# Two-layer four-mixer block: norms worked token tile by token tile, products around them reordered, both layers in one block

## The reference, cut to what matters

```
h = rmsnorm(x, n_pre_mix); proj = h @ w_in          # 1024 columns -> the branch inputs and gates
y_a .. y_d = four mixers (gated delta rule, dilated window attention, stick-breaking attention, retention)
mixed = (g_a*y_a + g_b*y_b + g_c*y_c + g_d*y_d) @ w_o
x = x + rmsnorm(mixed, n_post_mix)
h2 = rmsnorm(x, n_pre_mlp)
f = square(relu(h2 @ w_mlp_in)) @ w_mlp_out         # 1024 -> 4096 -> 1024
x = x + rmsnorm(f, n_post_mlp)
```

## Time and profile before

| what | value |
|---|---|
| median of three runs | 2524.46 us |
| the profiled execution: its own time | 2526.41 us |
| its span, first to last instruction | 2524.5 us |
| TensorE, share of the span | 95% |
| GpSimd, VectorE, ScalarE | 52%, 38%, 30% |
| mean granted TensorE clock | 0.979 of full speed |
| moved by DMA | 197.54 MB, mean 78 GB/s |

### The profile page before, as it was taken

The page is one execution under the profiler, slowest core; times in us unless marked ns, Lnnn a source line. Parts: engine busy times, 40 slices in busy tenths (PEclk is TensorE's granted clock), DMA queues, the critical chain, the costliest instruction groups (busy, mean ns, idle before and its releaser), DMA issues. The chain is left out here.

```text
span 2524.5 us, 29523 instructions
## 1 busy us (share of the span) xinstructions
PE 2386.9 (95%) x11488; PEld 1939.3 (77%) x11488; DVE 953.0 (38%) x1236; ACT 748.3 (30%) x1360; POOL 1319.0 (52%) x748
## 2 busy tenths in 40 slices
PE   7999999999998989999789999999999988999996
PEld 6798876777776768888677988768777766788885
DVE  4662325434634431123246632255246254212222
ACT  4434225222135121122144442351222341211221
POOL 4512653555643646677455126436555435566773
PEclk9999999999999999999999999999999999999998
DMA  4201321322221323322032013213222213232221
GB/s 158 84 26 34 92 84 50 108 83 86 63 70 44 104 80 93 100 93 99 26 110 84 18 43 92 75 50 117 75 88 68 69 44 100 84 96 96 97 95 50
DMA packets 107492, 197.54 MB, mean 78 GB/s; under 512 B 8528, under 2 KB 20816, under 8 KB 106960
## 3 DMA queue, kind: packets, MB, share of 16 engines
q1 hardware_dynamic: 106192, 189.27, 24.5%
q10 hardware_dynamic: 1152, 6.29, 0.7%
HBM read 193.44 MB, written 2.10 MB: 77 GB/s over the span
## 5 line engine op out<-in xcount | busy, mean ns | idle before, releaser
L507 POOL TENSOR_SCALAR ring_hi<-stage 128x1024 fp32r<-128x1024 f32 (+2 forms) x372 | 383.2, 1030 | 1137.8 <-PE big L1476 1085.2
L509 POOL TENSOR_TENSOR ring_lo<-stage,ring_hi 128x1024 fp32r<-128x1024 f32 (+2 forms) x372 | 936.8, 2518 | 31.0
L1476 PE MATMUL big<-h_hi,ring_hi 128*128 128x512 f32 (+1 forms) x1776 | 703.8, 396 | 4.2 <-POOL ring_lo L509 1.7
L1476 PE MATMUL big<-h_hi,ring_lo 128*128 128x512 f32 (+1 forms) x1776 | 693.6, 391 | 0.0
L1476 PE MATMUL big<-h_lo,ring_hi 128*128 128x512 f32 (+1 forms) x1776 | 693.6, 391 | 0.0
L1476 PEld LDWEIGHTS big<-h_hi,ring_hi 128*128 128x128 f32 (+1 forms) x1776 | 334.4, 188 | 81.2 <-issue 6.7
L1476 PEld LDWEIGHTS big<-h_lo,ring_hi 128*128 128x128 f32 (+1 forms) x1776 | 333.9, 188 | 71.6
L1476 PEld LDWEIGHTS big<-h_hi,ring_lo 128*128 128x128 f32 (+1 forms) x1776 | 334.3, 188 | 70.3 <-issue 1.9
L1476 PE MATMUL big<-ring_hi,h_hi 128*128 128x512 f32 x768 | 299.7, 390 | 6.2 <-DVE scr L1032 6.2
L1476 PE MATMUL big<-ring_lo,h_hi 128*128 128x512 f32 x768 | 298.8, 389 | 0.0
L1476 PE MATMUL big<-ring_hi,h_lo 128*128 128x512 f32 x768 | 298.8, 389 | 0.0
(11 more groups left out here) (239 smaller groups left out, 2434.8 us busy)
## 6 DMA issues: line engine op xcount, KB each, us to landing
stage<-in_w_in SPq DMA_DIRECT2D x168, 512.0 KB, 3.6
stage<-in_w_mlp_in SPq DMA_DIRECT2D x64, 512.0 KB, 3.8
stage<-in_w_mlp_out SPq DMA_DIRECT2D x64, 512.0 KB, 3.5
stage<-in_w_o SPq DMA_DIRECT2D x16, 512.0 KB, 3.5
stage<-in_w_br_a SPq DMA_DIRECT2D x8, 512.0 KB, 3.7
stage<-in_w_br_c SPq DMA_DIRECT2D x8, 512.0 KB, 3.5
stage<-in_w_br_d SPq DMA_DIRECT2D x8, 512.0 KB, 3.5
stage<-in_w_br_b SPq DMA_DIRECT2D x8, 512.0 KB, 3.4
```

The source lines that it names most:

```text
L507: nc.gpsimd.tensor_scalar(rH[jw][0:pp, r, 0:kk, 0:job.n], w, 1.0, 0.0, ALU.mult, ALU.add).then_inc(sem("w_hi"), 1)
L509: nc.gpsimd.tensor_tensor(rL[jw][0:pp, r, 0:kk, 0:job.n], w, f32(rH[jw][0:pp, r, 0:kk, 0:job.n]), ALU.subtract).then_inc(sem("w_ready"), 1)
L1476: ins_ = MM(o_, a_, r_, start=s0, stop=s1)
```

## The change

1. **One block.** The two layers are written out one after the other for every engine (`sync_layer`, `gpsimd_layer`, `scalar_layer`, `vector_layer`, `tensor_layer`). Semaphores are no longer cleared: `upto(name, count)` adds a fixed number per layer. Weights of layer 1 are loaded and split while layer 0 ends. Rotation matrices and most constants are loaded behind the first four weight units; the first DMAs are the identity, token tiles 0 and 1 and the small weights.
2. **Products by token.** `o1` and the last four units of `dn1` run with the token tile outermost: tile 0 through all four units, then tile 1, 2, 3. The output tiles of `o` and `dn` for tokens 0 and 1 lie in the big banks (o0 tile 0 in bank 0, o1 tile 0 in 1, o0 tile 1 in 2, o1 tile 1 in 3), those for tokens 2 and 3 in the mix banks.
3. **Norm chains by token tile.** Square, root, weighting (in PSUM), residual, square of x, root and split follow each other for one token tile of 128 tokens, and the next one's follow behind; the split takes 128 columns at a time.
4. **Scaled transposes.** The scaled copy `hn` is gone. TensorE multiplies the x block (float32) by a diagonal matrix `turn` of the tokens' roots, which VectorE makes from the identity, and so transposes and scales at once.
5. **Halves.** `aq` and `up0` run first for tokens 0 to 255 (products of 256 columns) through all four units, then for tokens 256 to 511.
6. **Output** is stored in four DMAs, one per token tile, each behind that tile's residual.
7. **Fills** of the window loop move from steps 1, 3, 5, 8 to 0, 1, 3, 6.

```diff
+    by_token(*[("pre1", t, hf) for t in range(2) for hf in range(2)])
     for j in JOBS:
+        if j.name in BY_TOKEN:
+            if j.name[-1] == "0":
+                by_token(*[(j.name[:-1] + str(hf), t) for t in range(2) for hf in range(2)])
+            if j.name == "o1":
+                by_token(*[("pre2", t, hf) for t in range(2) for hf in range(2)])
+            continue
...
+            def turned(tag, t):
+                pe.wait_ge(*upto(f"{tag}_dg", t + 1))
+                for hf in range(2):
+                    ps = tile_of((tag, t, hf))
+                    for q in range(4):
+                        k = 4 * hf + q
+                        i = MM(ps[:, q * P:(q + 1) * P], xv[:, t, k * P:(k + 1) * P], turn[:, t, :], start=True, stop=True)
+                    done(i, (tag, t, hf))
+            def normed(tag, t, i):
+                if i % 2:
+                    big_freed(pe, (tag, t, i // 2))
+                else:
+                    pe.wait_ge(*upto(f"{tag}_lo", 6 * t + 3 * (i // 2) + 2))
+            def halves(name, tag, turns):
+                for i in range(4):
+                    normed(tag, 1, i)
+                    for two in ((0, 1), (2, 3)):
+                        unit(job, i, two, slice(0, 2 * P))
+                        for t in turns.get((i, two[0]), ()):
+                            turned(tag, t)
+                for i in range(4):
+                    normed(tag, 3, i)
+                    unit(job, i, None, slice(2 * P, S))
+            def by_token(name, first_unit, tag, need=None):
+                for t in range(NT):
+                    for i in range(first_unit, len(job.units)):
+                        unit(job, i, (t,))
+                        if i == first_unit and t >= 2 and tag:
+                            turned(tag, t - 2)
...
             do("o0", lambda i: pe.wait_ge(*upto("m_lo", 2 * i + 2)))
-                do("o1")
-                pre("pre2")
-                for g in range(8):
-                    do(f"up{g}", None if g else pre_split("pre2"))
+            by_token("o1", 0, "pre2")
+            halves("up0", "pre2", {(0, 0): (2,), (2, 0): (3,)})
+            for g in range(1, 8):
+                do(f"up{g}")
...
-                    if i in (1, 3, 5, 8):
+                if i in (0, 1, 3, 6):
                     fill(1)
...
+            halves("aq", "pre1", {(0, 0): (2,), (2, 0): (3,)} if l else {(1, 2): (2, 3)})
...
+            def after_products(name, tag, ntag, nw, last):
+                for t in range(NT):
+                    y_square(name, 1, t, tag, 4)
+                    y_root(tag, t)
+                    if last:
+                        continue
+                    if t:
+                        split_hi(ntag, nw, t - 1, range(4))
+                    x_square(name, t, ntag)
+                    x_root(ntag, t)
+                    if t:
+                        split_hi(ntag, nw, t - 1, range(4, 8))
+            def diagonal(tag, t):
+                newton(p_y, p_t, p_h, tag, t)
+                TS(turn[:, t, :], ident, p_y[:, t:t + 1], None, ALU.mult).then_inc(sem(f"{tag}_dg"), 1)
...
+                for t in range(NT):
+                    for hf in range(2):
+                        big_freed(sp, (f"dn{hf}", t))
+                    sp.dma_start(x_out[:, t, :], xv[:, t, :]).then_inc(stored, 16)
```

More of the change, by code:

```diff
@@ L293, in mixer_keys @@
     k += [("bf", t) for t in range(5)]
-    k += [("pre2", i) for i in range(KT)]
+    k += [(f"o{hf}", t) for t in (2, 3) for hf in range(2)]
+    k += [("pre2", t, hf) for t in (2, 3) for hf in range(2)]
+    k += [(f"dn{hf}", t) for t in (2, 3) for hf in range(2)]
     return k
@@ L320, in hybrid_kernel @@
         lw = sb("lw", LEND)
-        st = sb("st", 320)
+        st = sb("st", 328)
         scr = sb("scr", 19968)
@@ L407, in sem, with upto @@
             return sems[name]
+        layer = [0]
+        def upto(name, count):
+            return sem(name), count + layer[0] * PER_LAYER.get(name, 0)
         x_loaded = [ctx.enter_context(nc.semaphore(f"x_loaded{t}")) for t in range(NT)]
+        ident_loaded = ctx.enter_context(nc.semaphore("ident_loaded"))
         consts_loaded = ctx.enter_context(nc.semaphore("consts_loaded"))
@@ new lines, in gpsimd_layer @@
+        def gpsimd_layer(pool, l):
+            layer[0] = l
+            for u, (job, i) in enumerate(UNITS):
+                r0, rows = job.units[i]
+                n = u + l * len(UNITS)
+                s, r = n % STAGES, n % RING
+                pp, kk = min(rows, P), max(rows // P, 1)
+                pool.wait_ge(sem(f"w_loaded{s}"), 16 * (n // STAGES + 1))
+                if u >= RING or l:
+                    pool.wait_ge(*upto("w_used", u - RING + 1))
+                w, jw = stg[job.width][0:pp, s, 0:kk, 0:job.n], job.width
+                nc.gpsimd.tensor_scalar(rH[jw][0:pp, r, 0:kk, 0:job.n], w, 1.0, 0.0, ALU.mult, ALU.add).then_inc(sem("w_hi"), 1)
+                pool.wait_ge(*upto("w_hi", u + 1))
+                nc.gpsimd.tensor_tensor(rL[jw][0:pp, r, 0:kk, 0:job.n], w, f32(rH[jw][0:pp, r, 0:kk, 0:job.n]),
+                                        ALU.subtract).then_inc(sem("w_ready"), 1)
@@ L1484, in do @@
-                def do(name, need=None, between=None):
-                    job = JOB[name]
-                    for i in range(len(job.units)):
-                        if need:
-                            need(i)
-                        unit(job, i)
-                        if between:
-                            between(i)
-                fills = []
-                def fill(n=1):
-                    for _ in range(n):
-                        if fills:
-                            unit(*fills.pop(0))
@@ L1502, in half_fill @@
-                def half_fill(t):
-                    unit(*(fills[0] if t == 0 else fills.pop(0)), (t,))
-                def set_fill(*names):
-                    assert not fills
-                    fills.extend((JOB[name], i) for name in names for i in range(len(JOB[name].units)))
-                order = iter([key for key in MIX if key[0] != "raw"])
-                def tile_of(key):
-                    assert next(order) == key, key
-                    b, k = MIX[key]
-                    if k > 1:
-                        pe.wait_ge(sem(f"mix_free{b}"), k - 1)
-                    return mxb[b]
```

2668 lines of the change are left out of this document (1375 added, 1293 removed), and 5 rows, old and new, of the table PER_LAYER.

## The result

The changed kernel took 2504.55 us (median of three runs, 2502.1 to 2505.26; a fourth run, disturbed to 12331.92 us, is left out), the kernel before beside it 2524.74. The ratio is 0.9918, with a 95% interval of 0.9899 to 0.9938. It is faster by 20.2 us at the medians, 0.8%, and that is clear of the scatter. Forecast were 40.2 us and a time of 2484.3 us; the measured time lies above the range of 2470 to 2502. In the profiled executions the span fell from 2524.5 to 2502.7 us; this execution took 2504.55 us in all.

The account below looks back on a forecast made before the run. TensorE, busy 95% of the span, was taken as the bound, with 137.6 us of rest to win. Terms 16.8 + 18.6 - 0.4 + 12.0 - 9.4 + 5.6 = 43.2, less 3.0, gave 40.2 us gained: 2484.3 us, range 2470 to 2502.

Parts of the forecast that it names:

- End: After the last product: residual and store by token tile take 7.5 us against 19.4, 12.0 us gained.
- o0's banks: At o0: new banks make TensorE wait 6.1 us for yb1's last tile, clock falls; 9.4 us lost over both layers.
- Rival C: Banks of o0 harmless, no clock lost or VectorE frees sooner, fills give their full 4; near 2477 us, chance 0.17.
- Fills: Window loop: moved fills remove a 2.06 us wait and its low clock; 2.8 us gained per layer, 5.6 in all.
- Mid-layer: Between o1 and up0: tile chains hide under products, 9.2 us against 17.6; 8.4 us gained per site, 16.8 in all.
- Boundary: Between the layers: same chain, no loop end, table load or repeated loads; 8.9 us against 27.5, 18.6 us gained.
- Launch: Kernel start: first product 4.7 us earlier, but transposes, halves and waits follow; 0.4 us lost.
- Margin: Taken off the sum: 1 us per site for late units or a held-up VectorE step, 3.0 us.
- Rival B: The ring: first slot returns only after the last tile's products, up0 and aq wait 5.3 us a site; near 2501, chance 0.08.
- Rival D: Slower: GpSimd's weight splits stretch VectorE's SBUF work in tiles 2 and 3, 15 us a site; 2530 us, chance 0.03.
- Rival A: At the sites: the chain by tile is longer than its cover, three sites lose 24 us; near 2508, chance 0.15.

Follow-up runs that it names:

- the fills' own run: Changed kernel with the window loop's fills back at rounds 1, 3, 5 and 8: 2508.18 us, ratio 0.9943 to the kernel before.
- the last kernel above: Changed kernel with all cures: o and pre2 banks reordered, one-element steps rewritten, launch root before tile 2's square, 20 products of ones first; 2464.80 us.
- the kernel with the diagonal on ScalarE: Changed kernel with newton's steps taking one tensor and per-partition numbers, and the diagonal made by ScalarE: 2494.76 us, ratio 0.9890 to the kernel before.

## Why the prediction was wrong, and the step that failed

The prediction had the mechanism of the gain and the sign, but the sum was some 20 us too large and the time fell outside the range. By its own steps, each from the profiled executions:

- **End, 12.0 us:** 12.9 measured from the last product on (19.4 less 6.5). Right. Counted from up1's first product in layer 1, it is 11.3 (334.8 us for 346.1): dn1 by token waits 0.88 us for the ring again, at 2478.20, and the prediction had this wait only in the boundary.
- **o0's banks, 9.4 us lost:** 5.89 and 5.87 us of wait, for the 6.1 worked out, where 3.1 stood before. Behind the wait nine products took 3.8 us instead of 2.0, so the clock cost some 1.7 us where the prediction had chosen 2.0. That is 4.5 us a layer and 9.0 together. Right, and the part of the change with the cheapest cure, one line. Rival C, harmless banks, is out.
- **Fills, 5.6 us:** 3.0 and 3.3 us in the two layers of the fills' own run. Right.
- **Mid-layer, 8.4 us a site:** 2.2 measured. This is the step that failed. Its transposes (6.8 us for 7.2) and halves (1.35 for 1.2) were right; its wait was 4.56 us instead of 0.8, and 2.7 us of slow clock came behind it. The step said that the diagonals of tiles 1 to 3 are ready 2 to 3 us before TensorE comes. For tile 2 three steps that take 0.7 us together took 5.2 beside GpSimd, which starts just then, since `o1` by token gives its ring slots back at the last tile. With up0's bank out of the way the diagonal was 1.83 us late; the bank, which the prediction had at 0.8, made 4.56 of it.
- **Boundary, 18.6:** 14.7 measured, from up1's first product to the first product of L1699 (394.0 us; 408.7 before, to L1545). The same three steps took 1.77, 0.97 and 2.47 us there.
- **Launch, 0.4 us lost:** 6.4 lost. The second turned tile was expected at 11.0 and came at 16.02. Tile 2's load, behind whose square the root of tile 1 stands on ScalarE, landed near 10.2 where the prediction estimated 8.6: some 1.5 us. Then newton and the diagonal of tile 1 took 0.74, 0.96 and 2.47 us beside GpSimd: 3.5 us. GpSimd begins at 8.97 instead of 13.54 because its load now comes sooner; the prediction had this load at 7.4 and did not ask what runs beside the split. An earlier load started the engine that holds the chain. The transposes were reckoned at full clock, 1.8 us each, and took 3.78.
- **Margin, 3.0 us,** for a VectorE step held up or a late unit: the mid-layer sites, the boundary and the launch missed 12.4, 3.9 and 6.0 us, together 22.3, seven times the margin.

The measured terms add up to 20.4 us, with 5.4 for the fills as these two executions have them. The profiled executions differ by 21.9. The other 1.5 us lie in stretches that the change does not touch, where the traces scatter.

Rival B, the ring, is out: up0's first unit was split at 891.53, when o1 ended at 891.67. The small pieces of the split did not decide anything in the layers either: L1116 takes 0.34 us a piece, as worked out.

With the one-element steps in their other form most of this comes back: the site by 6.1 us to 8.3 (8.4 forecast), the boundary by 2.7 to 17.4 (18.6), the launch by 4.1 us to 2.3 lost (0.4). So one uncounted mechanism is nearly all of the miss. That this kernel's 2484.29 us stands beside the forecast of 2484.3 so closely is luck: the launch still loses 1.9 us more than forecast, the boundary gains 1.2 less, the margin of 3.0 us was not needed, and the traces scatter by more than all of these. The launch's rest is not the slow transposes alone, since the last kernel above has them at full rate and its first product comes no sooner.

Rival D had named the mechanism and its place, tiles 2 and 3 beside GpSimd, and was kept out of the sum with a chance of 0.03, as a catastrophe of 45 us. It was there, at two fifths of the size (18 us). The argument against it was wrong: that one-column steps are short. A step that stands until the neighbour's instruction ends costs what is left of that instruction, up to 2.4 us, however short it is itself. The rows for this stood before the prediction: L1049 at 680 to 2893 ns and L509 with a median of 2397; the difference between the two ends of L1049 is 2.2 us, close to one GpSimd instruction. And the trace of the kernel before has a small step that is held, a VectorE step of 128x2 that takes 0.17 us alone and here ends with GpSimd's instruction:

```profile
729.27 1.05 POOL L507 TENSOR_SCALAR ring_hi<-stage 128x1024 fp32r<-128x1024 f32 x1 [8.16 <-PE big L1476]
729.48 0.88 DVE L1363 TENSOR_SCALAR st<-st 128x2 f32<-128x2 f32 x1
```

Rival A's price (2508) was near the time, and the chain was longer than its cover, as it says; but the cause was a hold of single steps and not the number of hand-overs.

## What to carry to other kernels

When a chain is moved under other work, ask for each of its steps which instruction will run beside it on GpSimd, and take a VectorE step with two tensors in SBUF, or a wide one from SBUF alone, at the whole length of that instruction; write steps of one element per partition with one tensor and per-partition numbers. A small step is not a short one: 128x2 steps were held as well. Give banks to a new job in the order in which the job before frees them, and ask the same of the next job's first tile. A rival that is a matter of degree belongs in the sum at its likely size, not only among the rivals at its worst.

## What was not expected of the hardware

- A `tensor_scalar` of 128x1 with two per-partition numbers from SBUF took 0.21 to 0.27 us beside GpSimd in every case seen, `scalar_tensor_tensor` of the same data up to 2.36 us (the variance's sum in the kernel with the diagonal on ScalarE) where it took 0.14 to 0.22 alone. A 128x128 `tensor_scalar` from SBUF is held (0.29 us became up to 2.48), though it has one tensor input, and so are those of 128x2 and 128x4 (0.17 us became 0.57 to 0.88). What sets the 128x1 apart was not tried.
- VectorE's steps are held by GpSimd's instruction of one input (L557, 1.05 us) as by that of two (L559, 2.4 us).
- TensorE began the launch at half its rate, 0.24 us for an instruction that elsewhere takes 0.12, while the granted clock in the profile's row was 1.00, because no record of the clock stands that early in the trace. Behind 28 other products it ran at full rate from the first turned tile on (1.95 us for the 16).
- Making TensorE quicker ahead of a wait can cost time: in the kernel with all cures 2.71 us of wait at the launch were followed by products at 0.65 of the clock.
